# Attention heads: the chunk mask as a scalar-engine copy over the scores instead of two accumulated matrix products

## The reference, cut to what matters

```python
cid = jnp.where(pos < N_META, 0, (pos - N_META) // CHUNK + 1)
...
s = jnp.einsum('bqhmd,bkhmd->bhmqk', qb, kf)
mask = cid[None, :] <= qc[:, None]
p = jax.nn.softmax(jnp.where(mask, s, NEG_INF), axis=-1)
a = p[:, :, 0] - lam * p[:, :, 1]
return jnp.einsum('bhqk,bkhe->bqhe', a, vf)
```

## Time and profile before

| | |
|---|---|
| median of 3 runs | 1548.88 us (1548.65 to 1548.92) |
| profiled execution | 1548.65 us, span 1546.9 us |
| PE busy (matmul) | 1524.8 us, 99% of the span |
| DVE busy | 1108.0 us, 72% |
| ACT busy | 664.2 us, 43% |
| products of L860 | 64 (8 heads, 4 blocks, 2 maps) |

### The profile page before, as it was taken

One profiled execution on the slowest core, in us unless ns is written; L12 is line 12 of the kernel. 1 busy time (PEld: TensorE's weight loads), 2 busy tenths in 40 slices (PEclk: granted clock), 3 DMA queues, 4 the chain that ended last, 5 costly groups with the idle time before them and its releaser, 6 DMA issues.

```text
span 1546.9 us, 25404 instructions
## 1 busy us (share of the span) xinstructions
PE 1524.8 (99%) x9972; PEld 1362.7 (88%) x9972; DVE 1108.0 (72%) x1590; ACT 664.2 (43%) x1035; POOL 34.3 (2%) x66
## 2 busy tenths in 40 slices
PE   7999999999999999999999999999999999999998
PEld 7999899998999999999988888878888888888887
DVE  5789888888565487777765458897748987777123
ACT  5324565656653343333433345744645332333112
POOL 0000000000000000000000020000000000000000
PEclk9999999999999999999999999999999999999999
DMA  6333122222233323233222353221132333232221
GB/s 178 82 82 110 55 56 78 60 71 67 55 83 97 94 83 108 81 84 105 64 83 86 104 123 78 61 73 50 55 108 57 100 93 106 81 108 96 109 82 55
DMA packets 235294, 131.63 MB, mean 85 GB/s; under 512 B 20920, under 2 KB 228676, under 8 KB 235220
## 3 DMA queue, kind: packets, MB, share of 16 engines
q1 hardware_dynamic: 234836, 130.40, 30.0%
q0 software_dynamic: 384, 0.20, 0.1%
HBM read 128.48 MB, written 2.10 MB: 84 GB/s over the span
## 4 chain that ended last, share of the span: by engine, by line
PE 87%; DVE 8%; ACT 4%; issue 1%; DMA 0%; DVEq 0%; ACTq 0%
PE psP L677 29%; PE psS L677 24%; PE psP L742 8%; PE psS L1358 4%; PE psP L1358 4%; PE psP L699 4%; PE psP L1049 3%; DVE conv L2070 3%; PE psP L1226 1%; PE psS L1226 1%; DVE wl L1961 1%; PE psP L896 1%; PE psP L805 1%; ACT wh L1410 1%; PE psS L853 1%
## 5 line engine op out<-in xcount | busy, mean ns | idle before, releaser
L1961 DVE TENSOR_TENSOR wl<-raw,wh 128x2048 fp32r<-128x2048 f32 x124 | 284.1, 2291 | 178.0 <-ACT wh L1410 176.6
L1410 ACT ACTIVATE wh<-raw 128x2048 fp32r<-128x2048 f32 x124 | 237.0, 1911 | 209.9 <-PE psS L1358 74.3
L677 PE MATMUL psP<-xh,wh 128*128 128x258 f32 (+2 forms) x1184 | 295.4, 312 | 3.5 <-ACT qkv L1504 1.5
L677 PE MATMUL psP<-xh,wl 128*128 128x258 f32 (+2 forms) x1184 | 291.6, 309 | 0.0
L677 PE MATMUL psP<-xl,wh 128*128 128x258 f32 (+2 forms) x1184 | 291.3, 309 | 0.0
L677 PE MATMUL psS<-xh,wh 128*128 128x258 f32 (+2 forms) x880 | 209.9, 305 | 0.4 <-DVE hT L1990 0.4
L677 PEld LDWEIGHTS psP<-xh,wh 128*128 128x128 f32 x1184 | 192.8, 190 | 18.3 <-issue 4.1
L677 PE MATMUL psS<-xh,wl 128*128 128x258 f32 (+2 forms) x880 | 208.5, 304 | 0.0
L677 PE MATMUL psS<-xl,wh 128*128 128x258 f32 (+2 forms) x880 | 208.1, 303 | 0.0
L677 PEld LDWEIGHTS psP<-xl,wh 128*128 128x128 f32 x1184 | 192.5, 189 | 12.0 <-issue 0.2
L677 PEld LDWEIGHTS psP<-xh,wl 128*128 128x128 f32 x1184 | 192.3, 189 | 11.9
(11 more groups left out here) (464 smaller groups left out, 2434.0 us busy)
## 6 DMA issues: line engine op xcount, KB each, us to landing
raw<-in_w_in_dram SPq DMA_DIRECT2D x76, 512.0 KB, 4.9
raw<-in_w_up_dram SPq DMA_DIRECT2D x44, 512.0 KB, 4.6
raw<-in_ffn_up_dram SPq DMA_DIRECT2D x44, 512.0 KB, 4.9
raw<-in_ffn_down_dram SPq DMA_DIRECT2D x22, 512.0 KB, 4.2
raw<-in_w_out_dram SPq DMA_DIRECT2D x16, 512.0 KB, 4.5
raw<-in_w_down_dram SPq DMA_DIRECT2D x16, 384.0 KB, 3.6
raw<-in_w_down_dram SPq DMA_DIRECT2D x16, 320.0 KB, 4.0
raw<-in_w_conv_out_dram SPq DMA_DIRECT2D x8, 512.0 KB, 4.6
```

The costliest lines, as they stand in the source:

```text
L677: ins = mm(ps[0:rows, a, 0:nn], W[:, s, half, k, 0:rows], Y[:, k, c0 + a * nn:c0 + (a + 1) * nn], start=(k == 0 and p == 0), stop=(k == KT ...
L1410: fn(wh[:, n % 2], raw[:, n % 2], ACT.Copy).then_inc(s_hi, 1)
L1961: V.tensor_tensor(wl[:, n % 2], raw[:, n % 2], wh[:, n % 2].bitcast(f32), ALU.subtract).then_inc(s_lo, 1)
```

## The change

The two products per block are gone. ACT gets a function `mask(a, t)` that waits for `scores_ready`, copies a constant tile `never` (64 partitions, 2 x 64, filled with -1e30) over the rectangle of both maps in PSUM, and tells a new semaphore `scores_masked`, on which the maxima now wait. In ACT's order `mask(a, 0)` and `mask(a, 1)` stand together ahead of `exps(a, 0)`, `mask(a, 2)` right ahead of `exps(a, 2)` and `mask(a, 3)` right ahead of `exps(a, 3)`. Six memsets of DVE at the start become one.

```diff
@@ PE, scores(a, t)
-                        mm(bank[:, 0:PW[t]], q, K[:, 0:PW[t]], start=True, stop=False)
-                        last.append(bank[:, PW[t] - 64:PW[t]])
+                        ins = mm(bank[:, 0:PW[t]], q, K[:, 0:PW[t]], start=True, stop=True)
...
-                        mm(scores_ps[:, 2 * m + 1, 0:HT], q, K[:, HT:T], start=True, stop=False)
-                        last.append(scores_ps[:, 2 * m + 1, HT - 64:HT])
-                for m, P in enumerate(maps):
-                    ins = mm(last[m], mki[P, :], mkk[P, :], start=False, stop=True)
+                        ins = mm(scores_ps[:, 2 * m + 1, 0:HT], q, K[:, HT:T], start=True, stop=True)
@@ ACT
+            def mask(a, t):
+                act.wait_ge(s_qk, 4 * a + t + 1)
+                if t < 3:
+                    hidden = scores_ps[0:64, 2 * (t % 2):2 * (t % 2) + 2, PW[t] - 64:PW[t]]
+                else:
+                    hidden = scores_ps[0:64, :, HT - 64:HT].rearrange("p (m a) b -> p m a b", m=2)[:, :, 1, :]
+                fn(hidden, never[:], ACT.Copy).then_inc(s_mk, 1)
...
                 if 0 <= a < NH:
+                    if a == 0:
+                        act.wait_ge(s_nv, 1)
+                    mask(a, 0)
+                    mask(a, 1)
                     exps(a, 0)
                     exps(a, 1)
...
                         copy_values(a)
+                    mask(a, 2)
                     exps(a, 2)
                     copy_probs(a, 0)
...
                         centred_squares(4, 6)
+                    mask(a, 3)
                     exps(a, 3)
@@ DVE
-            V.memset(mki[:].bitcast(f32), 0.0)
-            own(V.memset(mkk[:].bitcast(f32), 0.0))
-            for m in range(2):
-                V.memset(mki[64 * m:64 * m + 1, 0:64].bitcast(f32), 1.0)
-                V.memset(mkk[64 * m:64 * m + 1, :].bitcast(f32), -BIG)
+            V.memset(never[:], -BIG).then_inc(s_nv, 1)
...
             def maxima(a, t):
-                dve.wait_ge(s_qk, 4 * a + t + 1)
+                dve.wait_ge(s_mk, 4 * a + t + 1)
```

More of the change, by code:

```diff
@@ L224, in program @@
         var = at("var", [128, 2, TT + 1])
-        mki = at("mki", [128, 128], f32r)
-        mkk = at("mkk", [128, 64], f32r)
+        never = at("never", [64, 2, 64])
         ch = at("ch", [128, KT, S], f32r, start=base)
@@ L334, in program @@
         s_ex = sem("exps_ready")
+        s_nv = sem("mask_value_set")
+        s_mk = sem("scores_masked")
         s_cb = sem("probs_combined")
@@ L846, in scores @@
                 maps = [slice(64 * m, 64 * m + 64) for m in range(2)]
-                last = []
                 for m, P in enumerate(maps):
```

## The result

The changed kernel takes 1553.56 us (median of 8 executions, 1552.69 to 1555.11) against 1548.77 us before (again 8 executions); the ratio is 1.003, 95% interval 1.0021 to 1.0039. It is slower by 4.8 us. The forecast was 1553.7. The profiled execution took 1552.84 us (span 1551.0), 4.2 us more than the profiled one before.

The account below looks back on a forecast made before the run. PE, busy 99% of the span, was taken as the bound, its third quarter without slack towards ACT. Terms 5.0 + 0.4 - 0.3 = +5.1 us on the profiled 1548.65 gave 1553.7 us, range 1552.0 to 1555.8.

Parts of the forecast that it names:

- The place: Third quarter of turns 3 to 7: PE starts 0.15 us after ACT's copy, no slack, so ACT's delay reaches PE.
- Rival 2: Third quarter: ACT's delay finds slack, all 32 pairs come off PE, 1544.5 to 1547.6 us; chance 0.03.
- The queue: Block 2, turns 3 to 7: mask copy stands behind four value copies; of +1.00 us only 0.3 is the copy.
- The size per turn: Block 2, turns 3 to 7: maxima and PE +1.00 us later per turn, +5.0 in five; bounds 0.89 and 1.11 each.
- rival 1: PE gains 0.13 us per pair, ACT's copy costs 0.16 or overlaps: 1551.5 to 1552.1 us; chance 0.07.
- What PE saves: Mask products of blocks 0 and 1, turns 3 to 7: 0.033 us a pair, ten pairs, -0.3 us.
- Turn 8: Block 2 of turn 8: copy goes behind `empty(8, 0)`, maxima +0.99 us, PE's third quarter +0.4 us.
- Blocks 0, 1 and 3, memsets, the rest: Other blocks' copies, DVE's start memsets and later stages: covered by idle time or slack, 0 us.
- The total: Whole kernel: 5.0 + 0.4 - 0.3 = +5.1 us, giving 1553.7 us, 0.33% slower.

Follow-up runs that it names:

- not2: Changed kernel with the mask products kept for block 2 only, ACT copying for blocks 0, 1 and 3: 1548.49 us against 1548.77 for the kernel before.
- only2: Changed kernel with ACT's mask copy for block 2 only, blocks 0, 1 and 3 keeping their products: 1553.56 us against 1548.77 for the kernel before.
- early2: Changed kernel with block 2's mask copy moved between ACT's first value copy and the four small ones, turns 1 to 7: 1549.82 us against 1548.77 before.
- nomask: Kernel before without the 64 mask products and nothing in their place, so output differs: 1548.93 us against 1548.77.
- dve: Changed kernel with a DVE memset ahead of its maxima in place of ACT's mask copies: 1553.08 us against 1548.86 for the kernel before.
- behind: Changed kernel with ACT's mask copy after the maxima instead of ahead of them: 1555.28 us against 1548.86 for the kernel before.
- best_before: Kernel before (mask products) with ACT's norm and DVE's inversion moved behind the second weight split in turns 2 to 7: 1546.54 us against 1548.93.
- best_after: Changed kernel with norm and inversion moved behind the second weight split in turns 2 to 7: 1546.26 us against 1548.93 for the kernel before.
- after2: The changed kernel measured once more, unaltered, six executions: 1553.26 us against 1548.93 for the kernel before, ratio 1.003.

## Why the prediction was right, point by point

- *The place.* Right. PE starts the third quarter 0.14 to 0.15 after ACT's copy in turns 2 to 7, before and after; not2 and only2 put the loss on block 2, the norm's move takes it away. Rival 2 needed slack in that distance; there is none.
- *The queue.* Right: 0.3 for crossing and copy (early2), 0.6 for what stands in front.
- *The size per turn.* "I take 0.27. Then DVE starts its maxima at 217.87 + 0.01 + 0.27 + 0.04 = 218.19" was 0.15 too late. The copy took 0.25, and it started 0.09 before the end of the last small copy (217.76 against 216.76 + 1.09 = 217.85), where I had put it 0.01 behind. So 5 x 0.86, not 5 x 1.00. My bounds of 0.89 to 1.11 had missed that overlap; rival 1 had named it.
- *What PE saves.* 0.03 per pair, right by the steps in two traces (the changed kernel and nomask). Of the turns' 0.86, 0.08 comes back: 5 x 0.78 = 3.9, against 5.0 - 0.3 = 4.7 forecast. (By its rows, the 0.107 for 128 columns in the prediction is 0.11; the 0.03 comes out with either.)
- *Turn 8.* 0.4 forecast, 0.21 measured, for the most part by the same overlap: there the copy started at 389.53, 0.1 before `empty(8, 0)` ended:

```profile
389.03 0.60 ACT L1500 ACTIVATE u<-psP 128x516 f32<-128x516 f32 x1
389.53 0.26 ACT L1508 ACTIVATE psS<-never 64x128 f32<-64x128 f32 x1
```

- *Blocks 0, 1 and 3, memsets, the rest.* Nothing, as forecast: not2 for the blocks, and the 0.09 by turn 2 leaves no room for more. `gated` at the top of turn 3 starts at 206.58, 0.2 later than in the earlier trace rows, and PE's first quarter at 209.69 as before.

```profile
206.58 0.68 DVE L2149 SCALAR_TENSOR_TENSOR yT<-yT,psP 128x512 f32<-128x512 f32 x1
```

- *The total.* By the profiled executions my sum was 0.9 too high (+5.1 against +4.2). The median of the runs, +4.8, lies nearer to it only because half of them lie 1.4 us or more above the others, which the prediction knew nothing of. The number was right within its range; its closeness, 1553.7 against 1553.56, is luck.

## What to carry to other kernels

In this kernel an operation handed from a full engine to one that is 43% busy was priced by its place in the receiving queue. So look at what stands in front when its input is ready, and follow what hangs behind it to the next wait of the full engine, in every turn whose chain runs differently (turns 1, 2 and 8 decided dve and behind). Here 0.03 us of PE per block was traded for 0.86 us of delay in one block of four, while the other three were free. The chain ended at a wait without slack, and moving a long unrelated step out of it (the norm with its two table loads) was worth more than the trade, and made the trade harmless.

## What the runs showed of the hardware that was not expected

- In one profiled execution a wait of PE cost more than its length. In the profile of not2 the third quarter of turn 2 starts after a wait of 1.7 us, and there PE's granted clock is at 0.50, its lower level of 1.2 GHz; two products of 264 columns take 0.64 us, where the kernel before has 0.40 to 0.41:

```profile
191.81 0.74 PE L682 MATMUL psP<-xh,wh 128*128 128x264 f32 x2 [1.68 <-ACT qkv L1509]
192.36 0.64 PE L682 MATMUL psP<-xl,wh 128*128 128x264 f32 x2
```

  One stretch of the timeline, 3 us long (columns: length, then busy time and count of PE, PEld, DVE, ACT, POOL, then PE's granted clock, DMA share and GB/s), for not2 and for the kernel before:

```profile
191.90:194.90 3.00, 3.00 (x14) 3.00 (x15) 3.00 (x5) 1.14 (x6) 0.00 (x0) 0.50 0.00 0
```

```profile
191.90:194.90 3.00, 3.00 (x27) 3.00 (x27) 3.00 (x4) 1.17 (x3) 0.00 (x0) 1.00 0.03 5
```

  There are 14 products in place of 27. The clock is back within the next 3 us, and turn 3 of that execution is 1.5 us longer. The length of the wait alone does not decide: at the same place the clock stayed at 1.00 behind a wait of 1.53 in the kernel before, of 1.67 in the changed one, of 2.64 in dve and of 2.92 in behind.

  This fits the higher times. Of the 29 executions of the kernel before in the first series of experiments, 8 lie 1.6 to 2.3 us above most others and show a mean granted clock of 0.998 where the others show 0.999 or 1.0; so do 4 of the 8 of the changed kernel. That these have the cause seen in not2 was not shown, since none of them was profiled. Two executions of only2, 0.9 above the rest, show 1.0 and need another cause. And that the 22 executions of best_before and best_after, where the wait is gone, have no such times (1546.38 to 1547.18 and 1546.05 to 1546.96) proves little: on that chip the 22 executions of the kernel before had none either (1548.6 to 1549.47), though after2 had two of six.
- ACT overlapped the small copy from SBUF into PSUM with the copy before it by 0.1 us (217.76 against 217.85), whereas the four copies on 16 partitions ran end to end (1.09 for four of 0.27).
- Where ACT waits on a semaphore for its own copy, copy and wait took 0.31 from its start to the start of the exponentials (behind, turn 3).
